# First layer's output projection in one stage behind the heads, with the pool layer's weight products between its passes

## The reference, cut to what matters

```python
# layer 0
proj = x @ w_in                      # xm, z, o: 2048 columns each, gates: 16
xc = silu(causal_conv4(xm))          # q, k from xc, v from xm, per head of 256 columns
h  = mlstm_chunkwise(q, k, v, i, f)  # 8 chunks of 128 tokens, state carried
hb = sigmoid(o) * norm(h) + skip * xc
x  = layer_norm(ALPHA * x + (hb * silu(z)) @ w_out)
# layer 1
u, z = split(x @ w_in_pool)          # u: 4 groups of 512 columns
pooled = window_means(u) - u         # windows of 2, 4, 8, 16 tokens
mixed = einsum(pooled, w_group) * scale
x  = layer_norm(ALPHA * x + (mixed * silu(z)) @ w_out_pool)
```

## Time and profile before

| | us |
|---|---|
| median of 3 runs | 1603.43 (1602.33 to 1606.68) |
| profiled execution | 1602.14 |
| its span, first to last instruction | 1600.4 |
| PE busy | 1528.5 |
| DVE busy | 1068.1 |
| ACT busy | 568.8 |
| POOL busy | 286.5 |

### The profile page before, as it was taken

How to read it: one execution, slowest core, us unless ns; L and a number is a source line. 1 busy time by engine, 2 the same in 40 slices (tenths; PEclk the granted TensorE clock), 3 DMA queues, 4 the chain that set the end, 5 groups by cost and what they waited for, 6 DMA issues and landing times.

```text
span 1600.4 us, 20406 instructions
## 1 busy us (share of the span) xinstructions
PE 1528.5 (96%) x6994; PEld 1266.6 (79%) x6994; DVE 1068.1 (67%) x1623; ACT 568.8 (36%) x850; POOL 286.5 (18%) x195
## 2 busy tenths in 40 slices
PE   7999999999999999999999978979999999889998
PEld 6888888888888888888888856758887777768886
DVE  4867667567477477576675866645777777879424
ACT  5632422422422332323324345554443333343210
POOL 3302212213122122132032335310000000000001
PEclk9999999999999999999999989889999999999999
DMA  5112201202111112021112125642222222173121
GB/s 174 56 29 65 53 27 54 64 26 65 40 40 52 39 39 66 26 66 48 31 53 77 54 79 158 222 135 65 79 79 80 79 79 79 46 289 116 41 87 53
DMA packets 103911, 120.46 MB, mean 75 GB/s; under 512 B 5784, under 2 KB 81704, under 8 KB 103856
## 3 DMA queue, kind: packets, MB, share of 16 engines
q1 hardware_dynamic: 102784, 119.70, 23.8%
q10 hardware_dynamic: 1072, 0.07, 0.0%
HBM read 98.74 MB, written 21.00 MB: 75 GB/s over the span
## 4 chain that ended last, share of the span: by engine, by line
PE 85%; DVE 9%; DMA 2%; issue 2%; ACT 1%; POOL 1%; DVEq 0%; SPq 0%; ACTq 0%; POOLq 0%
PE wide L1765 23%; PE wide L1767 23%; PE wide L1766 23%; PE ps_intra L1907 2%; PE ps_inter L1910 1%; PE ps_state L1912 1%; DMA fold_raw<-in_pool_w_fold 1%; DVE blk L1558 1%; PE wide L1814 1%; DVE blk_raw L1572 1%; PE ps_s L1765 1%; PE ps_s L1900 1%; DVE win_a L1626 1%; PE ps_s L1766 1%; PE ps_s L1767 1%
## 5 line engine op out<-in xcount | busy, mean ns | idle before, releaser
L1765 PE MATMUL wide<-x_hi,w_hi 128*128 128x512 f32 x768 | 307.0, 400 | 0.0
L1767 PE MATMUL wide<-x_hi,w_lo 128*128 128x512 f32 x768 | 299.6, 390 | 0.0
L1766 PE MATMUL wide<-x_lo,w_hi 128*128 128x512 f32 x768 | 298.8, 389 | 0.0
L747 POOL TENSOR_TENSOR w_lo<-w_raw,w_hi 128x1024 fp32r<-128x1024 f32 x64 | 169.2, 2644 | 420.4 <-ACT w_hi L839 419.3
L1767 PEld LDWEIGHTS wide<-x_hi,w_lo 128*128 128x128 f32 x768 | 144.1, 188 | 31.0
L1766 PEld LDWEIGHTS wide<-x_lo,w_hi 128*128 128x128 f32 x768 | 144.5, 188 | 27.8
L1765 PEld LDWEIGHTS wide<-x_hi,w_hi 128*128 128x128 f32 x768 | 144.4, 188 | 27.4
L1766 PE MATMUL wide<-xa,blk 128*128 128x512 f32 x384 | 149.7, 390 | 0.0
L1765 PE MATMUL wide<-xb,blk 128*128 128x512 f32 x320 | 129.1, 403 | 16.4 <-DVE zz L1600 14.9
L1767 PE MATMUL wide<-xb,blk 128*128 128x512 f32 x320 | 127.3, 398 | 0.0
L1765 PE MATMUL wide<-w_hi,y_hi 128*128 128x512 f32 x256 | 102.0, 398 | 4.7 <-DVE y_lo L1278 4.7
(11 more groups left out here) (288 smaller groups left out, 3105.5 us busy)
## 6 DMA issues: line engine op xcount, KB each, us to landing
w_raw<-in_mlstm_w_in SPq DMA_DIRECT2D x48, 512.0 KB, 3.9
fold_raw<-in_pool_w_fold SPq DMA_DIRECT2D x32, 512.0 KB, 4.2
w_raw<-in_mlstm_w_out SPq DMA_DIRECT2D x16, 512.0 KB, 3.8
folded<-stage SPq DMA_DIRECT2D x32, 256.0 KB, 4.3
a_raw<-in_pool_w_z SPq DMA_DIRECT2D x16, 512.0 KB, 3.8
a_raw<-folded SPq DMA_DIRECT2D x16, 512.0 KB, 3.7
y_rows<-zz SPq DMA_DIRECT2D x16, 512.0 KB, 2.8
wo_raw<-in_pool_w_out SPq DMA_DIRECT2D x16, 512.0 KB, 10.3
```

The source lines that it names most:

```text
L747: link(pool, pool.tensor_tensor(w_lo[:, k % 2, :], w_raw[:, k % 2, :], w_hi[:, k % 2, :].bitcast(F32), ALU.subtract), lo_ready, s + 1)
L1765: pe.matmul(dst, a[0], b[0], start=first, stop=False, skip_group_check=more)
L1766: pe.matmul(dst, a[0], b[1], start=False, stop=False, skip_group_check=more)
L1767: return pe.matmul(dst, a[1], b[0], start=False, stop=last, skip_group_check=more)
```

## The change

- The output projection leaves the heads. Heads 1 to 7 lose `project`, its 16 residual adds, two weight slots and the split of y. The gated output is written into f_buf and stored to DRAM (`y_heads`), 256 KB at a time.
- DVE's order at the head of a later head becomes: three taps of the first tile's convolution, the gated output of the head before, the fourth tap and the rest.
- Behind the heads comes one list `STAGE`. The projection takes 3 passes over tokens (tiles 0 to 2, 3 to 5, 6 and 7), each with all 16 K tiles in PSUM (steps K: per token tile and half three matmuls, so 18, 18 and 12). w_out is loaded and split in the first pass and kept; y is loaded again from `y_heads` for each pass, through a ring of six. The residual with ALPHA is added once per tile.
- The pool weight products (steps F) are now by output tile: 32 units of 12 matmuls into one spare bank, from 256 KB of w_u and a group's w_group (1 MB, one buffer), split by ACT and DVE (in the last head by POOL). They stand between the K steps, as do the last head's transposes (T) and those of x (X, 8 of four tiles, then 16 of two).
- Both engines prepare operands four steps ahead (`LEAD`). The sums of x are made in halves by token, not by feature.

```diff
+USES_PER_HEAD = 24
+PASSES = ((0, 1, 2), (3, 4, 5), (6, 7))
+K_ORDER = (tuple(range(ET)), tuple(range(ET)), (4, 5, 0, 1, 2, 3, 6, 7, 9, 8, 10, 13, 14, 15, 11, 12))
+AFTER_K = {(0, 0): [("T", 0)], (0, 1): [("T", 1)], (0, 2): [("T", 2)], (0, 3): [("T", 3)], (0, 4): [("F", 3)],
+           (0, 6): [("F", 4)], (0, 8): [("F", 5)], (0, 10): [("F", 6)], (0, 12): [("F", 7)],
+           (0, 15): [("F", 8), ("F", 9)],
...
+           (2, 15): [*(("F", s) for s in range(24, 28)), *(("X", n) for n in range(16, 20)), ("F", 28),
+                     *(("X", n) for n in range(20, 24)), ("F", 29), ("F", 30), ("F", 31)]}
+STAGE = [("F", 0), ("F", 1), ("F", 2)]
-LATER = dict(xm=(0, 6), hn=2, out=8, z=24, q=28, k=32, v=(30, 31, 34, 35), o=36, s_xm=0, s_out=2, s_z=4, s_o=6, slots=8)
+LATER = dict(xm=(0, 6), hn=2, z=8, q=12, k=16, v=(14, 15, 18, 19), o=20)
...
 @block.sync
-                for n in range(2):
-                    load_slot(s0 + 2 + n, n, out_rows(w_out, h * DV - DV, n))
                 for j in range(2):
+                    load_slot(s0 + S_Z + j, j, in_cols(w_in, h * DV + (E + j * P)))
+                for m in range(4):
+                    sp.wait_ge(y_sum, h * 4 + (m - 3))
+                    sp.dma_start(y_heads[...], f_buf[:, m % 2, half(m // 2)]).then_inc(y_head_out, 16)
...
+            sp.wait_ge(wide_full, head_uses(HEADS - 1).full(LATER["o"] + 3))
+            for v in range(Y_RING):
+                load_wm(v)
...
+                load_ym(v)
...
 @block.scalar
                         if j == 0 and n == 1:
                             make_hi(s0 + 2, 0)
-                            if not first:
-                                prev_y(h - 1, range(3))
...
+            def mix_hi(v):
+                _, k, first = pass_of(v)
+                if first:
+                    act.wait_ge(w_out_in[k], 16)
+                    link(act, act.activation(wm[k][:, 0, :], wm_raw[k][:, 1, :], ACT.Copy), wm_hi, v + 1)
+                act.wait_ge(y_in[v % Y_RING], 16 * (v // Y_RING + 1))
...
 @block.vector
                 else:
+                    for f in work[:3]:
+                        f()
                     gated_output(h - 1, uses, [at["hn"] + m for m in range(4)])
-                    for n in range(2):
-                        for t in range(NC):
-                            residual(uses, at["out"] + n * NC + t, t, n)
-                            if t % 2 and len(work) > 2:
-                                work.pop(0)()
-                    for f in work:
+                    for f in work[3:]:
                         f()
...
+                        if not first and m == 0:
+                            dve.wait_ge(y_head_out, h * 64)
...
 @block.tensor
                 in_slot(uses, s0, 1, at["xm"][1])
-                if not first:
-                    project(uses, at["out"], s0, at["s_out"], h * 4 - 4)
...
+            def fold(s):
+                pe.wait_ge(fold_low, s + s // KT + 2)
+                r = s % WU_RING
+                for t in range(4):
+                    mm = split(spare_banks[spare_bank(("F", s))], [wu[:, r, i, tile(t)] for i in range(2)],
+                               [wg[:, i, t, :] for i in range(2)], t == 0, t == 3)
+                mm.then_inc(fold_full, 1)
+            def mix(v):
+                ts, k, first = pass_of(v)
+                j = v % ET
+                if first:
+                    pe.wait_ge(wm_lo, v + 1)
+                pe.wait_ge(ym_lo, v + 1)
+                for i, t in enumerate(ts):
+                    for n in range(2):
+                        if j == 0:
+                            mix_free(t, n)
+                        mm = split(mix_bank(t, n), [ym[:, v % Y_RING, part, tile(i)] for part in range(2)],
+                                   [wm[k][:, part, half(n)] for part in range(2)], j == 0, j == ET - 1)
```

More of the change, by code:

```diff
@@ L131 @@
 LATE = NC - 1
[L134 to L141, removed]
 def formed(n):
-    return (1, n - n // 4) if n % 4 else (0, n // 4 + 1)
+    on_act = n % 2 == 0
+    return (0 if on_act else 1), n // 2 + 1
 class Uses:
@@ L219, in build @@
             with ExitStack() as gates:
[L220 to L223, removed]
+                g_split = sb("g_split", [P, 2, SLOT], F32R, gates)
+            e_buf = sa("e_buf", [P, 2, S])
+            f_buf = sa("f_buf", [P, 2, S])
             qT = sa("qT", [P, S])
@@ new lines, in last_output @@
+            def last_output(m):
+                j, n = m % 2, m // 2
+                dve.wait_ge(turn_full, m + 1)
+                link(dve, dve.scalar_tensor_tensor(
+                    out=tmp_c[:, half(m % 2)], in0=spare_banks[spare_bank(("T", m))],
+                    scalar=cols[:, COL_G + ET - 2 + j:COL_G + ET - 1 + j], in1=e_buf[:, j, half(n)],
+                    op0=ALU.mult, op1=ALU.mult), turn_taken, m + 1)
+                link(dve, dve.tensor_tensor(f_buf[:, j, half(n)], tmp_c[:, half(m % 2)], f_buf[:, j, half(n)], ALU.add),
+                     y_sum, 4 * HEADS - 3 + m)
@@ new lines, in _ @@
+            for i, (kind, n) in enumerate(STAGE):
+                if i in PASS_END:
+                    for f in LO_STEP.get(i, ()):
+                        combined_lo(f)
+                    for t in PASSES[PASS_END.index(i)]:
+                        for c in range(2):
+                            mix_residual(t, c)
+                        mean(t, 0)
+                if kind == "T":
+                    last_output(n)
+                elif kind == "X":
+                    if n % 2:
+                        form_x(n)
+                    if n < KT and n % 2:
+                        for f in (n - 1, n):
+                            first_half_lo(f)
+                prepare(i + LEAD)
+                if i not in PASS_END:
+                    for f in LO_STEP.get(i, ()):
+                        combined_lo(f)
+                for t in NORM_STEP.get(i, ()):
+                    norm_tile(t)
+                for f in X_SUMS.get(i, ()):
+                    combine(f)
+                if (kind, n) == ("F", 28):
+                    block_lo(0)
+                    block_lo(1)
+                    for q in (7, 6, 3):
+                        add(0, q)
+                elif (kind, n) == ("F", 30):
+                    block_lo(2)
+                    block_lo(3)
+                    add(0, 5)
@@ L1591, in _ @@
             block_lo(4)
             block_lo(5)
+            for f in (8, 9):
+                combined_lo(f)
             def join(p, q):
@@ L1903, in outputs @@
                     if c == 0:
-                        for n in range(4):
+                        for n in (2, 3):
                             wait_taken(pe, uses, at["v"][n])
@@ L1992, in _ @@
+            for kind, n in STAGE:
+                if kind == "K":
+                    mix(n)
+                    continue
+                spare_free((kind, n))
+                if kind == "F":
+                    fold(n)
+                elif kind == "T":
+                    turn_last(n)
+                else:
+                    turn_x(n)
+            for b in range(4):
+                if b >= 2:
+                    pe.wait_ge(mix_taken, 2 * 6 + b - 1)
                 else:
-                    turn_x(i)
+                    evicted(*[step for step in SPARE if spare_bank(step) == b][-1])
```

708 lines of the change are left out of this document (355 added, 353 removed), and 6 rows, old and new, of the table AFTER_K.

## The result

Slower, as forecast, and by more. The changed kernel takes 1646.15 us (median of 4 runs, 1642.96 to 1649.82) against 1605.06 us of the kernel before beside it (4 runs): ratio 1.0256, 95% interval 1.0225 to 1.0287. Forecast were 1632 us and a range of 1598 to 1656. The profiled execution took 1649.82 us, with 1648.0 of span; before it was 1602.14 with 1600.4.

What follows compares the result with a forecast made beforehand. Heads were taken as bound by PE's matmuls, the bridge by waits. Span 1600.4 + 70 (heads) + 3 (last head) - 44.1 (bridge) = 1629.3 us; +28.9 on the median 1603.43 gives 1632 us, range 1598 to 1656.

Steps and rivals of the forecast that it cites:

- The first wait: Heads 1 to 7, bank 2: PE waits for the gated output behind three taps, 6.1 us a head.
- The bound of 4.1 us without the hold: Same wait at bank 2 if POOL's w_lo subtraction does not hold DVE's taps: 4.1 us a head.
- The second wait: Heads, behind the second input product: PE waits for the second xc_lo, 1.6 us a head, bounds 0 and 4.
- The clock: Heads: PE's matmuls run at low clock after the gap at bank 2, 2.3 us a head.
- 10 + 3: Last head: 10.0 us as in each head, plus 3 us for POOL's group weights holding DVE.
- The stage: New output stage: 6.5 us of PE waits left (bounds 3 and 25), a gain of 44.1 us.
- 3.5 us at the end: Stage's end: PE waits 3.5 us, DVE's some 36 us against PE's 29, part wanted only later.
- The start: Up to the first head's turns: the forecast sum has no term for it.
- (b): Bank 2, heads 1 to 7: POOL gives way, clock stays up, 1591 us; 1562 without the wait; chance 0.17 together.
- (c): Heads: no hold by POOL, but low clock, 4.1 + 1.3 to 2.7 us a head, 1600 to 1610; chance 0.10.
- (d): Stage bound by transfers or the ends: first pass 123 instead of 92 us, about 1663; chance 0.10.
- (e): Stage: the change fails its aim, waits stay as large as the bridge's 50 us, 1676; chance 0.03.

Runs made afterwards that it cites:

- run 1: Changed kernel with the gated output put back ahead of all convolution taps on DVE: 1589.44 us, ratio 0.9922.
- run 2: Kernel before, with only the gated output moved behind three convolution taps on DVE: 1665.83 us, ratio 1.0394.
- run 3: Changed kernel with one tap instead of three ahead of the gated output: 1601.94 us, ratio 0.9995.
- run 4: Changed kernel, taps still first, ACT's rounding that releases POOL's subtraction moved behind the third take of xm: 1634.48 us, ratio 1.0216.
- run 6: On run 5's kernel, the next head's qkv weights split (ACT rounding, POOL subtraction) in the core of the head before: 1565.49 us, ratio 0.9774.
- run 7: On run 1's kernel, without early tanh, the qkv weights split in the core of the head before: 1564.91 us, ratio 0.9775.
- run 8: Changed kernel, three taps still ahead, with only the qkv weights split in the core of the head before: 1621.95 us, ratio 1.0121.
- run 5: On run 1's kernel, ACT's tanh of the first tile moved ahead of two roundings: 1586.62 us, ratio 0.9907.
- run 9: On run 5's kernel, last group products' weights and sums in the stage's tail prepared sooner: 1591.23 us, ratio 0.9943; with the early qkv split too, 1570.25 us.
- run 10: On run 6's kernel, three of DVE's four sums of the first half cut to 256 of 1024 columns: 1566.12 us, ratio 0.9779.
- run 11: On run 7's kernel, DVE's four sums of the pool input and their low parts moved behind the residual: 1574.63 us, ratio 0.9825.

## Why the prediction was right, and where its numbers were off

The sign, the mechanism and the place were right; 1632 was 14 us under the median. The medians differ by 41.1 us. In the profiled execution, the slowest of its four, the span grew by 47.6 us against 28.9 forecast. The difference of 19 us splits up by the prediction's own terms; some of it, in the start and in the low clock, differs from execution to execution.

**The first wait, 6.1 us a head: measured 6.2** (5.4 in the last head, 758.79 us). Shown: the order alone makes it (runs 1, 2), its length is that of the taps ahead (run 3), and 2.1 us of it are POOL's hold (run 4). The bound of 4.1 us without the hold was met to the tenth. Reading the hold off the same POOL instruction beside L1266 in the earlier trace rows was sound. The Trainium skill, "SBUF — State Buffer", section "Who interferes with whom", whose rule was weighed there, is borne out by the 3.38 us tap, which was not slowed in proportion but stopped until POOL was done.

**The second wait, 1.6 us: measured 2.0.** The prediction let one of POOL's two subtractions fall on the chain; both did, on tap 0 (1.8 us) and on f_buf (1.3 us), which with its 1 us of slack makes 2.1. That POOL's subtractions are the cause, on a chain that has lost the projection's cover, is shown by runs 2 and 6 to 8; putting tanh ahead in ACT's order took only 0.2 us a head off (run 5).

**The clock, 2.3 us a head: measured 1.5 + 1.7 = 3.2.** This is the mis-sized term of the heads. The 2.3 was taken for the first gap alone, from the earlier trace rows. It was too high for this execution (1.6 on the mean of seven), though run 2 lost 2.2 behind the same wait. The second, short gap was given no low clock at all. It had one in six of seven heads here, but in run 1 the same gap had it in two, where it made a head 0.4 us longer; so it isn't a price of this gap by itself, and what it depends on is not shown. In sum 11.7 a head instead of 10.0. The last head lost 7.6 where 10 + 3 were forecast: a shorter second wait (1.18 us at 795.39), which leaves nothing for a hold by POOL's group weights.

**The stage, 6.5 us of waits: measured 17.9** (292.92 against 275.0 of PE's work). That is the largest miss, 11.4 of the 19 us. Up to 1093 us the reasoning held: 0.68 us before the first K step, none at the changes of the group weights, transfers beside PE. The "3.5 us at the end" failed. PE waits 2.16 + 1.01 + 0.19 + 3.03 + 1.71 = 8.1 us there, and 26 matmuls run at 0.43 us behind the waits, 5.4 us more:

```profile
1093.65 0.67 PE L1849 MATMUL wide<-wg,wu 128*128 128x512 f32 x1 [2.16 <-DVE wu L1561]
...
1109.48 0.77 PE L1849 MATMUL wide<-wg,wu 128*128 128x512 f32 x1 [3.03 <-DVE wu L1561]
```

Of the rest 0.9 are the waits for wm and ym; some 3 to 4 us of the 17.9 I can't place. The prediction compared DVE's work with PE's as sums, 36 against 29 us, and took most of the difference to be work that is wanted later. But "four steps ahead" is 16 us of cover where the steps are K steps and under 2 us where they are the turns of x, and the weights of the unit behind those turns stand on ACT and DVE behind everything that the pass's end releases. And no low clock was put beside the waits; but the low clock isn't what makes the tail long. In runs 3 and 7, which have the same stage, it stood behind only one of these waits (1.7 us lost), PE waited 11.0 and 10.9 us instead of 8.1, and the stage took 292.2 and 292.1 us instead of 292.9. What PE gains in clock it waits longer for ACT and DVE. Runs 9 to 11 show that no single entry of this queue is the price: taking away one wait moved it (9, 10), and a late transfer in ACT's queue sat behind the next (11). What the best order would be is open.

**The start, nothing: measured 3.1 us,** 2.0 of it by the last turns of x. The change needn't be the cause: run 4, with the changed kernel's start, has 132.76 us to the turns of head 1 and run 2, with the old one, 138.31, where the two kernels have 136.55 and 133.49.

**Rivals.** (b) and (c), no long hold and no hold by POOL, are refuted by the tap of 3.38 us and by run 4; their price without the hold was right, but POOL doesn't give way. (d), transfers as the bound, is refuted for the stage's body (100.00 of 100.00 us busy at 178 GB/s). In the tail ACT does wait for one load, in the changed kernel as in run 11:

```profile
1096.72 0.63 ACT L1002 ACTIVATE wu<-wu_raw 128x512 fp32r<-128x512 f32 x1 [4.05 <-DMA wu_raw<-in_pool_w_u]
```

(e) is refuted by a gain of 32.6 us.

## What to carry to other kernels

When an engine's in-order queue is rearranged, ask of each entry which PSUM bank it frees and when its next writer comes: putting three others ahead of it cost 57 us here, and taking them away again turns a change that loses 2.6% into one that wins 0.8%. Work that is taken out of a place was also cover: here the projection had hidden a chain of DVE that was too long only with POOL's subtractions on it, and moving one of these into a stretch where DVE idles was worth 20 to 22 us in the heads (21 to 24 in the medians). In the tail of a stage count cover in microseconds of the actual steps, not in steps, and look for the chain on the other engines before pricing PE's waits one by one. A saving is best read from the stretch that was edited: up to 7 us of a difference stood elsewhere.

## What the runs showed of the hardware that I had not expected

- The same wait is followed by low clock in one execution and not in another. In the changed kernel nine matmuls came every 0.43 us behind each of six waits of 1.96 to 1.98 us for xc_lo (694.18 to 697.93 us: 1.7 us lost), as much as behind its waits of 6.20 us (657.18 to 660.3: 1.5). Waits of the same 1.96 to 1.99 us had it in two of six heads in run 1 and in one of six in run 3, and those of 1.71 to 1.76 us in run 5 in none. In the pool layer, where nothing was edited, two waits of 2.94 us were each followed by 14 matmuls at the low clock in the changed kernel (2.9 us lost; at 1353.81 and 1398.20 us), and by none in run 7 (1276.08 and 1317.58):

```profile
1353.81 0.77 PE L1849 MATMUL wide<-xb,blk 128*128 128x512 f32 x1 [2.94 <-DVE zz L1684]
1354.37 0.63 PE L1850 MATMUL wide<-xb,blk 128*128 128x512 f32 x1
```

```profile
1276.08 0.47 PE L1860 MATMUL wide<-xb,blk 128*128 128x512 f32 x1 [2.94 <-DVE zz L1695]
1276.39 0.40 PE L1861 MATMUL wide<-xb,blk 128*128 128x512 f32 x1
```

  All waits for tmp_c of 3.4 us and more (changed kernel, runs 2, 4 and 8) were followed by low clock, and none of 0.8 to 1.25 us (run 3). What decides in between is not shown.
- DVE's TENSOR_SCALAR of 1024 columns with a single tensor as input, 0.81 us alone, takes 2.60 us when POOL's subtraction has begun (675.39 and 674.14 us; 620.72 and 620.35 in run 5), as much as the two-input taps. The Trainium skill, "SBUF — State Buffer", section "Who interferes with whom", counts this operation among those that can take the shared port pair; the trace agrees.
- POOL isn't free in these meetings either: its subtractions of 2.34 to 2.46 us took 2.94 to 3.29 in the second wait's head where DVE was inside an operation with two inputs when they began (674.14 us, 0.18 behind xc's gate at 673.96: 3.29; 687.13: 2.94; 693.33: 3.03).
